# Rotary rotation of differential attention's queries and keys: from a copied stage to the projection's PSUM tile

## The reference

```
q_d = dq.reshape(B, N, H_D, 2, DK_D)          # 4 heads, 2 maps, 64 features: 512 columns
k_d = dk.reshape(B, N, H_D, 2, DK_D)
if latent:
    q_d = _rope(q_d, cos_d, sin_d)
    k_all = concat([cached, _rope(k_d, cos_d, sin_d)])
# _rope: x1, x2 = halves of the features
#        (x1 * c - x2 * s, x1 * s + x2 * c)
```

## Time and profile before

| | us |
|---|---|
| median of 3 runs | 2726.61 |
| lowest, highest | 2721.86, 2736.12 |
| the profiled execution | 2724.43 |
| its span, first to last instruction | 2722.6 |
| TensorE busy | 94% of the span |
| GpSimd, VectorE, ScalarE busy | 49%, 43%, 27% |
| mean granted clock of TensorE | 0.981 of full speed |

### The profile page before, as it was taken

The page is one execution under the profiler, slowest core; times in us unless marked ns, Lnnn a source line. Parts: engine busy times, 40 slices in busy tenths (PEclk is TensorE's granted clock), DMA queues, the critical chain, the costliest instruction groups (busy, mean ns, idle before and its releaser), DMA issues.

```text
span 2722.6 us, 41674 instructions
## 1 busy us (share of the span) xinstructions
PE 2570.2 (94%) x17328; PEld 2390.7 (88%) x17328; DVE 1177.5 (43%) x1692; ACT 741.9 (27%) x1332; POOL 1329.1 (49%) x604
## 2 busy tenths in 40 slices
PE   4999989999999999999979999999999999999997
PEld 3889976877999899999968899668689998999997
DVE  4443255777225423133554524559642273132233
ACT  3251335225311312021123512440433123021121
POOL 2535530440666566666644455005136665666663
PEclk8999999999999999999989999999999999999999
DMA  6102224530222122222211122342012222222221
GB/s 252 63 31 69 72 72 154 193 109 9 70 78 69 64 71 77 78 70 78 74 51 54 36 72 72 111 154 78 31 39 71 73 69 66 73 78 70 78 78 55
DMA packets 62556, 215.34 MB, mean 79 GB/s; under 512 B 6688, under 2 KB 11168, under 8 KB 62112
## 3 DMA queue, kind: packets, MB, share of 16 engines
q1 hardware_dynamic: 56448, 203.97, 22.3%
q10 hardware_dynamic: 5920, 8.70, 0.9%
HBM read 208.15 MB, written 4.49 MB: 78 GB/s over the span
## 4 chain that ended last, share of the span: by engine, by line
PE 82%; DVE 7%; issue 3%; ACT 2%; DVEq 2%; DMA 1%; POOL 1%; ACTq 1%; SPq 1%; POOLq 0%
PE big L465 22%; PE big L468 22%; PE big L469 22%; PE big L620 4%; PE last_two L651 2%; PE two L634 2%; PE last_two L547 1%; PE big L488 1%; DVE cols L1377 1%; PE big L491 1%; PE big L492 1%; DMA first_mod<-in_first 1%; DVE sq L1719 1%; DVE act_lo L1763 1%; DVEq L1685 1%
## 5 line engine op out<-in xcount | busy, mean ns | idle before, releaser
L433 POOL TENSOR_TENSOR w_hi<-raw,cst 128x1024 fp32r<-128x1024 f32 x288 | 556.1, 1931 | 1261.6 <-PE big L465 1133.1
L465 PE MATMUL big<-act_hi,w_hi 128*128 128x320 f32 x2784 | 869.3, 312 | 19.8 <-ACT stage L1229 6.4
L468 PE MATMUL big<-act_lo,w_hi 128*128 128x320 f32 x2784 | 862.6, 310 | 0.0
L469 PE MATMUL big<-act_hi,w_lo 128*128 128x320 f32 x2784 | 862.3, 310 | 0.0
L436 POOL TENSOR_TENSOR w_lo<-raw,w_hi 128x1024 fp32r<-128x1024 f32 x288 | 742.4, 2578 | 40.9
L465 PEld LDWEIGHTS big<-act_hi,w_hi 128*128 128x128 f32 x2784 | 525.0, 189 | 30.2 <-issue 26.8
L468 PEld LDWEIGHTS big<-act_lo,w_hi 128*128 128x128 f32 x2784 | 525.3, 189 | 0.9
L469 PEld LDWEIGHTS big<-act_hi,w_lo 128*128 128x128 f32 x2784 | 524.8, 189 | 0.0
L465 PE MATMUL big<-u_hi,w_hi 128*128 128x320 f32 (+1 forms) x1024 | 320.2, 313 | 12.7 <-DVE cols L1811 10.8
L468 PE MATMUL big<-u_lo,w_hi 128*128 128x320 f32 (+1 forms) x1024 | 318.7, 311 | 0.0
L469 PE MATMUL big<-u_hi,w_lo 128*128 128x320 f32 (+1 forms) x1024 | 318.3, 311 | 0.0
(11 more groups left out here) (304 smaller groups left out, 3459.7 us busy)
## 6 DMA issues: line engine op xcount, KB each, us to landing
raw<-in_w SPq DMA_DIRECT2D x368, 512.0 KB, 3.5
first_mod<-in_first SPq DMA_DIRECT2D x16, 512.0 KB, 15.7
x<-in_x ACTq DMA_DIRECT2D x1, 2560.0 KB, 13.0
out_y<-x SPq DMA_DIRECT2D x8, 320.0 KB, 2.3
cst<-in_const ACTq DMA_DIRECT2D x1, 1664.0 KB, 10.9
small<-in_small ACTq DMA_DIRECT2D x2, 437.0 KB, 9.2
out_C<-c_new ACTq DMA_DIRECT2D x2, 258.0 KB
v_d<-in_past ACTq DMA_DIRECT2D x2, 256.0 KB, 3.1
```

Source lines behind the costliest of these rows:

```text
L433: nc.gpsimd.tensor_tensor(w_hi[:, to, :], raw[:, slot, :], ones[:, 0:1].to_broadcast([P, BLK]), ALU.mult)
L465: first = mm(ps, wh, ah, start=k == 0, stop=False)
L468: mm(ps, wh, al, start=False, stop=False)
L469: last = mm(ps, wl, ah, start=False, stop=k == nk - 1)
```

## The change

ScalarE's eight copies to the stage are gone, in each layer, and with them its waits for the tiles and for VectorE's rotations. Its two copies of a modulation row stand one behind the other now. VectorE waits for the tile itself. It reads it in PSUM in two parts, because the latent columns lie in both banks: columns 128 to 320 (192 wide) and 320 to 640 (320 wide). Each part has one product with the cosines and four with the sines, in an instruction of two multiplications, of which the first is the scale. So there are ten products where there were five. The context columns are copied with the scale, and that instruction, the last that reads the tile, releases the PSUM buffer. The sum of `t1` and `t2` is as before. A drain stands behind the wait for the tile. The counts of `raw_kept` are 3 per layer now.

```diff
@@ ScalarE
-                for m in range(8):
-                    use = USE["dq"][m]
-                    wait_ready(act, l, use)
-                    act.wait_ge(roped, l * 11 + 3 + max(m - 1, 0))
-                    t, b, _ = buf(use)
-                    f(two_parts(stage[:, m % 2, :]), halves(t), ACT.Copy, scale=DK_D ** -0.5 if m < 4 else 1.0)\
-                        .then_inc(free[b], 1)
-                    act.drain().then_inc(raw_kept, 1)
-                    if l + 1 < DEPTH and m in (4, 7):
-                        keep_row(l + 1, m // 7, one[0][:, 0:256])
+                if l + 1 < DEPTH:
+                    keep_row(l + 1, 0, one[0][:, 0:256])
+                    keep_row(l + 1, 1, one[0][:, 0:256])
                 act.wait_ge(roped, l * 11 + 11)
@@ VectorE, the latent attention's rotary parts
-                    dve.wait_ge(raw_kept, l * 11 + j + 1)
+                    dve.wait_ge(raw_kept, l * 3 + j + 1)
...
-                dve.wait_ge(raw_kept, l * 11 + 3)
+                dve.wait_ge(raw_kept, l * 3 + 3)
@@ VectorE, this stage
                 for m in range(8):
-                    dve.wait_ge(raw_kept, l * 11 + 3 + m + 1)
+                    use = USE["dq"][m]
+                    wait_ready(dve, l, use)
+                    dve.drain()
+                    t, b, _ = buf(use)
                     dst = q_d[:, m, :] if m < 4 else k_d[:, m - 4, :]
-                    src = stage[:, m % 2, :]
-                    v.tensor_tensor(t1[:, CTX:T], src[:, CTX:T], c_("cos_d"), ALU.mult)
-                    for g in range(4):
-                        r, o = slice(32 * g, 32 * g + 32), slice(32 * (g ^ 1), 32 * (g ^ 1) + 32)
-                        v.tensor_tensor(t2[o, CTX:T], src[r, CTX:T], c_("sin_d", r), ALU.mult)
-                    v.tensor_copy(dst[:, 0:CTX], src[:, 0:CTX])
+                    scale = DK_D ** -0.5 if m < 4 else 1.0
+                    for a, z, src in ((CTX, HALF, t[:, 0, CTX:HALF]), (HALF, T, t[:, 1, 0:HALF])):
+                        v.scalar_tensor_tensor(t1[:, a:z], src, scale, c_("cos_d")[:, a - CTX:z - CTX], ALU.mult, ALU.mult)
+                        for g in range(4):
+                            r, o = slice(32 * g, 32 * g + 32), slice(32 * (g ^ 1), 32 * (g ^ 1) + 32)
+                            v.scalar_tensor_tensor(t2[o, a:z], src[r], scale, c_("sin_d", r)[:, a - CTX:z - CTX],
+                                                   ALU.mult, ALU.mult)
+                    v.tensor_scalar(dst[:, 0:CTX], t[:, 0, 0:CTX], scale, None, ALU.mult).then_inc(free[b], 1)
                     dve.drain()
                     v.tensor_tensor(dst[:, CTX:T], t1[:, CTX:T], t2[:, CTX:T], ALU.add)
                     dve.drain().then_inc(roped, 1)
```

## The result

The changed kernel takes 2730.5 us (median of 20 runs, 2725.3 to 2737.1). The kernel before, run beside it, takes 2725.1 us (20 runs, 2719.2 to 2736.1). The ratio is 1.002, with a 95% interval of 1.0011 to 1.0029: 5.4 us slower, 3.0 to 7.9. That is within the 0.5% that the prediction called no change, and it was forecast as +3.7. The profiled execution has a span of 2729.6 us at a mean granted clock of 0.977 (before: 2722.6 at 0.981).

The account below looks back on a forecast made before the run. TensorE, busy 94% of 2722.6 us, was taken as the bound, so only its waits count. Layer 0 (-1.3 + 3.9 + 2.0 = +4.6) and layer 1 (-0.9) gave +3.7 us: 2729 us, range 2720 to 2742.

Parts of the forecast that it names:

- The price of the products: VectorE's rotation products reading PSUM: 353 ns at 192 columns, 487 at 320; a tile's reads 4.66 us until release.
- The upper bound from the update of x: Dearer price for VectorE's PSUM products, 409 and 543 ns: reads take 5.2 us and a rotation 6.1.
- The waits: TensorE ahead of the value projection: new stall of 3.9 us in layer 0; 4.9 instead of 5.75 in layer 1.
- The modulation row: Layer 0, behind tile 4: TensorE's wait for ScalarE's row copy goes, -1.3 us.
- The rotation: VectorE's rotation of one tile takes 5.5 us, a single one up to 7.6, so VectorE stops being late.
- Tiles 0 to 6 cost nothing: Projections in both layers: buffers released before TensorE asks, as long as a rotation is shorter than a tile's 7.04 or 8.2 us.
- The clock behind layer 0's wait: TensorE's clock falls to 0.50 behind layer 0's new stall, slowing matmuls: 1.7 to 2.6 us, taken as 2.0.
- ScalarE's busy time: Whole kernel: falls by 11 us as ScalarE's 16 stage copies go, worth nothing by itself.
- The sum: Whole kernel: layer 0 +4.6 us, layer 1 -0.9, together +3.7 us; time 2729 us.
- (a): Rival: tile release held up less, or no low clock in layer 0; +1.7 us, 2727; chance 0.22.
- (b): Rival: GpSimd's splits hold up the new products, VectorE becomes the bound, rotations 9.5 us; about 2754; chance 0.05.
- (c): Rival: no stall at the value projection, layer 1's whole loss comes back; -1.3 - 8.2, 2715; chance 0.05.

Follow-up runs that it names:

- experiment 4: Changed kernel, but tile 7's and every tile's PSUM buffer released behind the last sum, not the context columns' copy: 2732.5 us against 2724.9 for the kernel before, ratio 1.0027.
- experiment 1: Changed kernel, but ScalarE copies tile 7 to the stage again in both layers: 2719.3 us against 2724.9 (0.9978), second series 2717.3 against 2726.8 (0.9965).
- 5: Changed kernel, but ScalarE copies tile 7 to the stage again in layer 0 only: 2722.7 us against 2726.5 for the kernel before, ratio 0.9985.
- experiment 6: Kernel before, with only the first modulation row's copy moved ahead of ScalarE's wait for tile 4: 2726.0 us against 2726.5, ratio 1.0.
- experiment 7: Changed kernel run again unaltered, 2734.8 us against 2726.5 (1.0024), and a second profile of the unaltered kernel before, span 2721.1 us.
- experiment 3: Kernel before with ScalarE's copies kept, VectorE's products in the new two-part form on the SBUF stage: 2732.8 us against 2724.9, ratio 1.0027.
- experiment 2: Changed kernel, but value projection takes token tiles 2, 3, 4, 0, 1 and awaits tile 7's buffer only before tile 0: 2721.8 us against 2724.9, 0.9982.
- experiment 8: Changed kernel, with unused matmuls (25 in layer 0, 32 in layer 1) on TensorE during the value projection's wait: 2727.3 us against 2726.8, ratio 1.0007.

## Why the prediction was right, point by point

- **The price of the products.** 353 and 487 ns were taken from the line through 256, 512 and 640 columns; 354 and 487 came. The reads were put at 4.66 us and took 4.64. The upper bound from the update of x wasn't needed. Nor was the estimate of 0.7 us more per rotation that the prediction worked out from the Trainium skill, VectorE: DVE Perf Modes, section on the TRN2 errata: the trace after doesn't show it (4.64 us for the reads).
- **The waits.** 3.9 and 4.9 were forecast; 3.84 and 4.85 came, released by the copy of the context columns, as experiment 4 shows by moving the release. The loss of the copy as cover for the last tile is shown by 1 and 5.
- **The modulation row.** -1.3 was forecast, and the idle time went. By experiment 6 the cause is the order of ScalarE's copies.
- **The rotation.** 5.5 us was forecast for most. In layer 1 all eight took 5.4 us (one from 1855.15 to 1860.59). In layer 0 the first seven took 6.1 to 6.6 (one from 513.16 to 519.55), because the last sum, with both inputs in SBUF, is still held up:

```profile
517.89 1.66 DVE L1720 TENSOR_TENSOR q_d<-t,sq 128x512 f32<-128x512 f32 x1
```

That was inside the bound of 7.6 and costs nothing, since the buffer is free before it.
- **Tiles 0 to 6 cost nothing.** No idle time stands between the projections in either layer.
- **The clock behind layer 0's wait.** It fell, as in the likelier case. The term was 2.0 us (1.7 to 2.6 as its bounds) and 2.35 came. The working for whether it falls was thinner than its result. It compared idle times of 3.22 (no fall) and 3.14 (fall), as if the length decided. Two executions of the same kernel differ behind the same 3.22 us, so the length alone doesn't, and one trace couldn't have told. For a wait of this length the traces speak more clearly: in the three executions that have it, of 3.84, 3.83 (experiment 7) and 4.60 us (experiment 4), the clock fell each time. The prediction had no idle time between 3.22 and 4.62 us to go by.
- **ScalarE's busy time.** -11 was forecast, -10.8 came.
- **The sum.** +3.7 was forecast. With the terms as measured it is -1.42 + 3.91 + 2.35 - 0.9 = +3.9. The runs give +5.4 (3.0 to 7.9), so the two agree. The waits alone are +1.6 of it (-1.34 + 3.84 - 0.9), and with every kernel put at one clock the changed one is +2.1 (± 1.1), which fits the waits apart from the clock. That leaves 3.3 us. The changed kernel's mean granted clock was 0.9776 in these runs. That of the kernel before isn't on record for them; in the series of the experiments it was 0.9789 to 0.9791. By the slope this is 2.1 to 2.5 us, the size of the fall behind layer 0's wait (2.35). The last 1 us isn't shown to be of the change.
- **The rivals.** (a), no fall, would have been +1.7 to its +3.7 and isn't what the trace shows. (b), new products held up, fell: none was over 495 ns. Its price of a held-up rotation, 9.5 us, is about what experiment 3 shows (9.6). The 27 us that it made of it weren't tried: experiment 3 lost 7, but with ScalarE's copy of tile 7 only six rotations stand ahead of the value projection, and in (b) all of them would. (c), no wait, fell as the code said. But its price of -8.2 in layer 1 was about the right size for what a kernel without the wait gains: together with -1.3 it gave 2715, and experiment 1, which keeps 0.84 us of it, measured 2719 and 2717.

What stays open: what decides whether the clock falls behind a given idle time, and whether a kernel with other waits gets other chances of it elsewhere. The changed kernel has more low stretches in its profiles than the kernel before, also in stages that the change doesn't touch (1728 to 1742 in the second). Two profiles of each can't tell whether that is chance.

## What to carry to other kernels

A copy out of PSUM that looks useless, on an idle engine and hidden for seven tiles of eight, can still be the shortest way to free the buffer, and the tile to look at is the last one, behind which someone wants all the buffers at once. Take such a copy away tile by tile: here taking away seven of eight gave 6 to 9 us (1.3 of them, by the trace, from the earlier copy of the modulation row), and the eighth cost 11 to 15. And where the bounding engine must wait, ask whether it can start on what is already free: changing the order of the consumer (experiment 2) took the same wait away without a copy.

## What the runs showed of the hardware

- **The granted clock after an idle time isn't the same from one execution to the next.** Behind 3.22 us it was 1.00 in one and 0.50 in another execution of one kernel (experiment 7), and behind 1.69 us it was 1.00 and 0.50 in the same two. Within one kernel, each 0.001 less of mean granted clock went with 1.65 ± 0.09 us more time (a straight line through all runs, each kernel and series with its own height). That line takes in two thirds of the variance of the runs of a kernel, which spread by 5 to 18 us. So a difference of 4 us needs many runs of both kernels, and a single pair of profiles here was 7.0 us apart where some 4 were the change.
- **Matmuls that compute nothing kept the clock up** through a wait of 3.9 and of 4.9 us (experiment 8). That gives back only what the clock cost, 3.5 to 4.6 us; taking the waits away gave 10 to 15 (experiments 1 and 2).
- **VectorE's products are held up beside GpSimd's splits with both inputs in SBUF and not with one of them in PSUM**: 345 to 2611 ns, against 346 to 495 (experiment 3 and the profile after). The copy of the context columns has a single input, and it was held up too while that lay in SBUF. First the copies of the queries' tiles in the kernel before, then in the changed one:

```profile
L1720 DVE COPY q_d<-stage x8: 226/228/2345, 512.3 to 1878.1; 128x128 f32<-128x128 f32 x8
```

```profile
L1718 DVE TENSOR_SCALAR q_d<-big x8: 292/292/293, 509.5 to 1873.6; 128x128 f32<-128x128 f32 x8
```
